# Expert gate and up weights laid out as rows 4p+k on partition p, in a two-layer attention and mixture-of-experts block

## What is computed

```python
h = rms_norm(x, norm_ffn_g[l])
g_logits = h @ w_rg + b_rg                     # 4 groups
e_logits = h @ w_re + b_re                     # 16 experts, 4 in a group
# the best group, its two best experts, softmax weights -> gate [seq, 16]
hid = silu(einsum('bsd,edf->bsef', h, w_g)) * einsum('bsd,edf->bsef', h, w_u)
hid = hid * gate[..., None]
x = x + einsum('bsef,efd->bsd', hid, w_d)
```

## Time and profile before

| | |
|---|---|
| median of 3 runs | 1417.36 us (1416.01 to 1417.49) |
| span of the profiled execution | 1414.7 us |
| instructions | 19421 |
| TensorE matmul | 1380.1 us busy, 98% |
| GpSimd | 762.0 us, 54% |
| VectorE | 747.1 us, 53% |
| ScalarE | 501.9 us, 35% |
| SP's DMA queue (q1) | 136030 packets, 197.59 MB, 43.4% of 16 engines |
| all DMA | 148567 packets, 224.26 MB, mean 159 GB/s |

### The profile page before, as it was taken

One profiled execution on the slowest core, in us unless ns is written; L12 is line 12 of the kernel. 1 busy time (PEld: TensorE's weight loads), 2 busy tenths in 40 slices (PEclk: granted clock), 3 DMA queues, 4 the chain that ended last, 5 costly groups with the idle time before them and its releaser, 6 DMA issues.

```text
span 1414.7 us, 19421 instructions
## 1 busy us (share of the span) xinstructions
PE 1380.1 (98%) x6804; PEld 1014.5 (72%) x6804; DVE 747.1 (53%) x1917; ACT 501.9 (35%) x1194; POOL 762.0 (54%) x643
## 2 busy tenths in 40 slices
PE   7999999999999999999889999999999999999997
PEld 5788877777777866656477887777777778665563
DVE  4487856656684155222146787675658543452221
ACT  4322333433432143334243332334343412343331
POOL 4566654454445625676545575544444554266763
PEclk9999999999999999999899999999999999999999
DMA  5435322223312758999732243222322147689995
GB/s 153 127 101 172 118 79 82 74 70 102 88 61 75 278 198 288 322 348 339 197 115 77 69 121 90 80 63 84 84 95 78 61 143 267 234 272 332 329 345 133
DMA packets 148567, 224.26 MB, mean 159 GB/s; under 512 B 18634, under 2 KB 95876, under 8 KB 148462
## 3 DMA queue, kind: packets, MB, share of 16 engines
q1 hardware_dynamic: 136030, 197.59, 43.4%
q0 software_dynamic: 9936, 16.81, 5.0%
q10 hardware_dynamic: 2496, 8.52, 1.5%
HBM read 215.47 MB, written 31.25 MB: 174 GB/s over the span
## 4 chain that ended last, share of the span: by engine, by line
PE 91%; DVE 4%; ACT 1%; issue 1%; POOL 1%; DMA 1%; SPq 0%; POOLq 0%; DVEq 0%; ACTq 0%
PE bank L859 20%; PE bank L861 18%; PE bank L860 18%; PE bank L1154 16%; PE bank L1035 4%; PE bank L1047 3%; PE bank L1068 2%; PE bank L1116 2%; PE bank L988 1%; PE bank L1058 1%; DVE probs L1849 1%; PE bank L1001 1%; POOL w_lo L733 1%; DVE mixed L1666 1%; PE bank L1126 1%
## 5 line engine op out<-in xcount | busy, mean ns | idle before, releaser
L727 POOL TENSOR_SCALAR w_hi<-raw 128x1024 fp32r<-128x1024 f32 (+2 forms) x142 | 148.7, 1047 | 418.1 <-PE bank L861 415.3
L733 POOL TENSOR_TENSOR w_lo<-raw,w_hi 128x512 fp32r<-128x512 f32 (+2 forms) x288 | 359.1, 1267 | 16.4 <-ACT w_hi L1579 4.6
L860 PE MATMUL bank<-w_hi,hT_lo 128*128 128x512 f32 (+2 forms) x696 | 258.5, 371 | 0.0
L1154 PE MATMUL bank<-work,ptmp 128*128 128x512 f32 x512 | 225.5, 592 | 1.0 <-ACT ptmp L1515 1.0
L859 PE MATMUL bank<-w_lo,hT_hi 128*128 128x512 f32 (+2 forms) x576 | 216.2, 375 | 2.4 <-DVE hT_lo L1674 1.0
L861 PE MATMUL bank<-w_hi,hT_hi 128*128 128x512 f32 (+2 forms) x576 | 211.6, 367 | 0.0
L1154 PEld LDWEIGHTS bank<-work,ptmp 128*128 128x128 f32 x512 | 94.6, 190 | 107.6 <-issue 106.2
L795 POOL TENSOR_TENSOR w_lo<-work,w_hi 128x512 fp32r<-128x512 f32 x120 | 148.1, 1263 | 43.0 <-ACT w_hi L1531 43.0
L859 PE MATMUL bank<-hT_lo,w_hi 128*128 128x512 f32 x384 | 159.5, 415 | 0.0
L861 PE MATMUL bank<-hT_hi,w_hi 128*128 128x512 f32 x384 | 150.7, 393 | 0.0
L860 PE MATMUL bank<-hT_hi,w_lo 128*128 128x512 f32 x384 | 150.1, 391 | 0.0
(11 more groups left out here) (308 smaller groups left out, 2342.7 us busy)
## 6 DMA issues: line engine op xcount, KB each, us to landing
work<-in_w_ff_gate SPq DMA_DIRECT2D x66, 512.0 KB
work<-in_w_ff_up SPq DMA_DIRECT2D x66, 512.0 KB
work<-in_w_ff_down SPq DMA_DIRECT2D x33, 1024.0 KB, 6.7
raw<-in_w_gate SPq DMA_DIRECT2D x48, 512.0 KB, 3.9
raw<-in_w_in SPq DMA_DIRECT2D x40, 512.0 KB, 3.5
raw<-in_w_branch SPq DMA_DIRECT2D x24, 512.0 KB, 3.6
raw<-in_w_out SPq DMA_DIRECT2D x16, 512.0 KB, 3.7
normed_dram<-mixed ACTq DMA_DIRECT2D x8, 512.0 KB, 2.7
```

Source lines behind the costliest of these rows:

```text
L727: nc.gpsimd.tensor_scalar(w_hi[:, two, :, 0:w], raw[:, slot, :, 0:w], 1.0, 0.0, ALU.mult, ALU.add).then_inc(split_hi, 1)
L733: last = nc.gpsimd.tensor_tensor(w_lo[:, two, kk, 0:w], raw[:, slot, kk, 0:w], w_hi[:, two, kk, 0:w].bitcast(F32), ALU.subtract)
L860: nc.tensor.matmul(out_ap, s_lo, m_hi, start=False, stop=False)
L1154: last = nc.tensor.matmul(G[e % 2][:, :], et[:, e % 2, kt * P:(kt + 1) * P], work[:, n % RING, kk, :], start=(kt == 0), stop=(kt == KT - 1))
```

## The change

Row 4p+k of a half of 512 rows now lies on partition p, for k from 0 to 3. The four rows of a partition are neighbours in DRAM, 4096 bytes in one run, and they also lie in one run in SBUF: a slot holds first all four gate rows of 256, then all four up rows. A gate matmul reads two pieces of 256 columns that are 4096 bytes apart. Block 4a+k of the turned rows must then hold columns 512a+4p+k of the model. So ScalarE writes the normalised rows in that column order, reading X with a stride of four elements. The gain in the same order is loaded into a new tile, `ffn_gain`, once for both layers, by two small DMAs behind the parameters of layer 0; `pcol` still serves the router. Waits on these loads are added on ScalarE (before the rows) and on VectorE (before the first expert). The overflow block's loads and matmuls change in the same way.

```diff
+        ffn_gain = sb("ffn_gain", [P, DEPTH, KT])
...
+        def in_expert_order(rows):
+
+            return rows.rearrange("p (a n k) -> p a k n", a=2, k=4)
+
+        def gate_up_piece(slot):
+
+            return work[:, slot].rearrange("p k n -> p (k n)").rearrange("p (h k n) -> p h k n", h=2, k=4)
...
             parameters(0)
+            for m in range(DEPTH):
+                sp.dma_start(ffn_gain[:, m, :].rearrange("p (a k) -> p a k", k=4),
+                             layer_of(norm_ffn_g, m).rearrange("l (a p k) -> p (l a) k", a=2, k=4)
+                             ).then_inc(gains_in, 16)
...
                             src = layer_of(w, l)[:, EXPERT_AT[e], part * 512:(part + 1) * 512, :]
-                            sp.dma_start(work[:, slot, :, half * FF:(half + 1) * FF],
-                                         src.rearrange("a (k p) n -> p (a k) n", p=P)).then_inc(piece_in[slot], 16)
+                            sp.dma_start(gate_up_piece(slot)[:, half],
+                                         src.rearrange("a (p k) n -> p (a k) n", p=P)).then_inc(piece_in[slot], 16)
...
                         last = nc.tensor.matmul(G[e % 2][:, :], et[:, e % 2, kt * P:(kt + 1) * P],
-                                                work[:, n % RING, kk, :], start=(kt == 0), stop=(kt == KT - 1))
+                                                gate_up_piece(n % RING)[:, :, kk, :], start=(kt == 0),
+                                                stop=(kt == KT - 1))
...
                     last = nc.scalar.activation(et[:, e % 2, q * P:(q + 1) * P], src, ACT.Copy,
-                                                scale=pcol[:, ROW_FFN + q:ROW_FFN + q + 1])
+                                                scale=ffn_gain[:, l, q:q + 1])
...
                 act.wait_ge(rs_done, TT + 1)
+                act.wait_ge(gains_in, 16 * DEPTH)
                 for t in range(TT):
-                    nc.scalar.activation(xn[:, t, :], X[:, t, :], ACT.Copy, scale=row_rs[:, 1, t:t + 1]).then_inc(xn_done, 1)
+                    nc.scalar.activation(xn[:, t, :].rearrange("p (a k n) -> p a k n", a=2, k=4),
+                                         in_expert_order(X[:, t, :]), ACT.Copy,
+                                         scale=row_rs[:, 1, t:t + 1]).then_inc(xn_done, 1)
                     act.wait_ge(xn_done, 2 * TT + t + 1)
                     act.dma_start(xn_dram[t * P:(t + 1) * P, :], xn[:, t, :]).then_inc(xn_out, 16)
...
                     et[:, e % 2, 512:1024].rearrange("p (q n) -> p q n", q=4), S[1][:, :].rearrange("p (q n) -> p q n", q=4),
-                    pcol[:, ROW_FFN + 4:ROW_FFN + 8].unsqueeze(2).broadcast_to([P, 4, P]), ALU.mult)
+                    ffn_gain[:, l, 4:8].unsqueeze(2).broadcast_to([P, 4, P]), ALU.mult)
...
             def experts():
+                v.wait_ge(gains_in, 16 * DEPTH)
                 et_out(0)
```

More of the change, by code:

```diff
@@ L356, in hybrid_block @@
         pre_eids = sem("pre_eids")
+        gains_in = sem("gains_in")
         par = sem("par")
@@ L1638, in over_act @@
                             last = nc.scalar.activation(et[:, 0, q * P:(q + 1) * P], S[0][:, q * P:(q + 1) * P],
-                                                        ACT.Copy, scale=pcol[:, ROW_FFN + q:ROW_FFN + q + 1])
+                                                        ACT.Copy, scale=ffn_gain[:, l, q:q + 1])
                         last.then_inc(e_et, 1)
@@ L2235, in over_dve @@
                                                            S[1][:, q * P:(q + 1) * P],
-                                                           pcol[:, ROW_FFN + 4 + q:ROW_FFN + 5 + q], None, ALU.mult)
+                                                           ffn_gain[:, l, 4 + q:5 + q], None, ALU.mult)
                         last.then_inc(e_et, 1)
```

## The result

The change made the kernel slower: 1422.88 us, median of 4 runs (1420.64 to 1422.98), beside 1416.93 (1416.01 to 1417.49) for the kernel before on the same chip. The ratio is 1.004, 95% interval 1.0025 to 1.0054. The forecast was 1417.9 and no measurable change; the result lies above the range's end of 1421.0. The profiled execution has a span of 1418.8 us (before 1414.7) and took 1420.64, so a run's time is 1.84 us above its span. It is the fastest of the four; the others took 1422.82 to 1422.98, so this trace explains the first 4.1 us of the loss and not what the median has beyond them.

What follows compares the result with a forecast made beforehand. TensorE, at 98% of the span, was taken to bound the kernel. Terms 0 + 0 + 0 + 0.5 + 0 gave +0.5 us on the median of 1417.36, so 1417.9 us, range 1415.2 to 1421.0.

Steps and rivals of the forecast that it cites:

- Part 1: Gate and up transfers in the expert stage: 0 us on the path, DMA share from 1.02 to about 0.8.
- Part 2: TensorE's matmuls beside less busy DMA engines: taken as 0, with -2.2 us kept as an end.
- Part 3: Gate matmul's moving operand in two runs of 256 columns: taken as 0, at the other end 1.4 us.
- Part 5: Two small loads of the gains in SP's queue: 0 with 5 us of slack, up to 2.7 us without.
- Part 4: ScalarE's normalising operation, four a layer, reading 16 bytes apart: taken as +0.5 us reaching TensorE.
- full doubling: Upper end for ScalarE's strided read: 0.85 us more an operation, 3.4 us over four, together +3.1 us.
- the signs that I had set for being wrong: Expert interval of 10.72 changes, layer 1's gap ahead of the turn passes 2 us, or a gap opens before 35 us.
- Slack in layer 0: Lateness of the last store that layer 0 absorbs before TensorE's turn waits: 1.2 + 1.7 = 2.9 us.
- the smaller slack of 0.8: Lower end of the lateness that layer 1 absorbs between last store and TensorE's turn: 0.8 us.
- the larger of 1.4: Upper end of the lateness that layer 1 absorbs between last store and TensorE's turn: 1.4 us.
- the rival's formula: Loss over both layers for a last store s late: (s - 0.8) + (s - 2.9).
- late gather: Rival: strided ScalarE elements cost double, so TensorE waits for gathered rows in both layers; 1420.5 us, chance 0.14.

Runs made afterwards that it cites:

- run 2: The change with ScalarE writing the normalised rows in order again, their columns not reordered to match the weights; 1416.55 us, ratio 1.0000.
- run 1: The change as it is, measured once more beside the others on one chip; 1422.14 us, ratio 1.0037.
- run 3: The kernel before with only ScalarE's strided read of X added, weights in their old order; 1420.61 us, ratio 1.0033.
- run 4: The change with ScalarE reading X in order and writing elements 512 bytes apart; 1420.84 us, ratio 1.0033.
- run 10: The kernel before with the first 768 columns of each tile of normalised rows written twice, nothing strided; 1421.76 us, ratio 1.0032.
- run 6: The kernel before with the first 512 columns of each tile of normalised rows written twice, nothing strided; 1418.51 us, ratio 1.0013.
- run 7: The kernel before with four ScalarE read orders, one a tile: elements 8 or 32 bytes apart, pairs 16 or 32 apart; one execution, 1415.72 us.
- run 11: The change with extra matmuls ahead of the turn of expert 0's gathered rows: six in both layers, 1421.55 us; eight in layer 1 alone, 1420.78 us.
- run 9: The change with rows 2p+k of a quarter on partition p: runs of 2048 bytes, ScalarE reading 8 bytes apart; 1417.38 us, ratio 1.0000.
- run 8: The change with GpSimd writing two of the four tiles of normalised rows by the same strided read; 1426.11 us, ratio 1.0074.

## Why the prediction was wrong, point by point

**Part 1, transfers: right on the path, wrong in size.** 0 us, as far as run 2's ratio can tell, and 98,423 packets. But the DMA share of the stage is 0.96 and 0.92, not 0.8. I had priced a 4096-byte packet at 146 ns, from a stretch with little other traffic. In 560 to 640 us of the change SP's queue spends 77.7% of sixteen engines on 6136 packets, 162 ns each; by the megabyte it spends 43.6 us of engine time now and 46.7 before, 7% less where I had counted on about 20%. Cover of the stage by TensorE held: 10.72 us.

**Parts 2, 3 and 5: right in sum.** The expert interval is the same to 0.01 us, and run 2 has the less busy DMA engines, the split operand and the gains' loads in it at a ratio of 1.0000. No run has one of them without the others, so a small gain by one and a small cost by another that cancel are not ruled out.

**Part 4, the strided read: the term that failed.** It took 0.26 to 0.6 us more an operation from VectorE's rows, and so +0.5 us in the sum. ScalarE's own is 0.98 us more, 3.9 over four; it lies just above the end that I had kept as full doubling (0.85, 3.4). Two of the signs that I had set for being wrong were read off at once: the operation took 2.13 us, not 1.4 to 1.75, and the gap in layer 1 passed 2 us. The chain behind the term was right in kind. Slack in layer 0 was put at 2.9 us: 3.9 late less 2.9 is 1.0, measured 1.1 to 1.3 where the clock stayed up [runs 1, 3, 4, 10]. In layer 1 the smaller slack of 0.8 gives 3.1 and the larger of 1.4 gives 2.5; measured 2.2 to 2.6. So the larger one was right. That the rival's formula with 3.9 gives 3.1 + 1.0 = 4.1 us, just what the spans differ by, is partly luck: in the trace layer 0 leaves 1.55 us to layer 1, more than the formula's 1.0, and layer 1 adds 2.4, less than its 3.1. The last store in run 6 was 2.8 us late, inside the slack of layer 0, and that layer showed no wait. Behind the turn of layer 0 another 0.4 us is lost by expert 1's first gate matmul (531.39 against 529.47, where the turn was 1.5 late); run 10 shows the same, so it too comes with lateness. By layer 1 as much has been made up again.

The rows that I took the stride from could not have shown it. They have 16 to 64 elements an operation, where the fixed part is most of the time, and they are another engine's. The sign of the Trainium skill's rule, page "SBUF — State Buffer", section "Specifications (TRN2)", that each 16-byte line wants two hits, was right, and the trace of run 7 agrees: 1.22 to 1.27 us with two elements of a line used, 2.29 with one, and 2.13 in the change. I gave it a rival's 0.14 and the weight went to the rows. Between two ends whose price only another engine's rows give, the end that the mechanism itself names deserved the larger chance.

**The rival "late gather" came true.** At doubling it gave 1420.5; the lower group of executions, 1419.8 to 1421.1, agrees. Its condition (0.8 us an operation) was met.

**What no case had: the clock in the new wait.** A wait of over 2 us was priced at its length. Half of the executions cost more than that, and the median of the change falls into that group. This, and not the waits alone, took the result out of the range: 1416.93 plus the 4.1 us of the traces is 1421.0, the range's end, and with the 1.4 us of run 10's trace it is 1422.4; measured 1422.88. That the 1.4 us belongs to the change's upper three executions is inferred from runs 4, 10 and 11, not seen in a trace of the change, and where the last half microsecond goes stays open. The other runs' medians (1420.61 to 1422.14) depend on how many executions fell into either group.

## What to carry to other kernels

Where ScalarE reorders as it reads, use at least two float32 elements of each 16-byte piece; here that took the price from 0.98 us to 0.07 an operation (runs 7 and 9). Striding the write instead was no way out (run 4); a write in pairs wasn't tried. Before giving a reordering to an engine, follow its result to the next store and gather, and compare the lateness over all tiles with the slack, layer by layer. Larger DMA runs bought nothing here, where TensorE was busy without a gap, and where a new wait is left on TensorE, price what its clock does behind it too.

## What the runs showed of the hardware that I hadn't expected

- ScalarE, 1024 float32 a partition, read from elements 8 bytes apart 1.22 us, 16 bytes 2.13, 32 bytes 2.29, pairs 32 bytes apart 1.27, in order 1.15. Read in order and written 512 bytes apart it takes 2.13 as well.
- TensorE with a stationary operand at 16 bytes: 32 products of 128x128 take 7.5 to 7.7 us instead of 3.8, a group of eight turns 1.12 instead of 1.04.
- GpSimd takes 3.9 us for the strided tile, and one operation of VectorE's ranking beside it took 2.02 us instead of 0.19 (in layer 1 another took 2.19 instead of 0.21), while its neighbours took their usual time.
- With four times fewer and larger packets for the gate and up weights, SP's queue spends 7% less of the DMA engines' time on a megabyte, at 332 to 336 GB/s.
- The granted clock falls to its lower level for some 3 us in some executions, and for nearly 7 us behind the waits of 2.9 and 2.8 us in run 8. Ahead of a wait for the gather the fall was absorbed; behind one it cost 1.4 and 1.6 us, in run 8 some 2.2 to 2.4 a layer.
